# Two transformer blocks on one core: normalisations ahead of the feed-forward layers one token tile behind the other, and four smaller reorderings

## The reference

```python
# first block
x = layer_norm(ALPHA * x + mixed, ln_mix)            # "x1"
x = layer_norm(ALPHA * x + cross_attention(x), ln_x) # "x2"
x = layer_norm(ALPHA * x + conv_ffn(x), ln_ffn)      # "x3"
# second block
y = concat([mlstm(x), dilated_attention(x)]) @ w_out
x = layer_norm(ALPHA * x + y, ...)                   # "x4"
x = layer_norm(ALPHA * x + memory_cross_attention(x, mem), ...)  # "x5"
x = layer_norm(ALPHA * x + swiglu_ffn(x), ...)       # the output

def conv_ffn(x, w_in, conv_w, conv_b, w_out):
    gate, up = split(x @ w_in, 2)                    # 5632 columns each
    gate = causal_conv(gate, conv_w) + conv_b        # 3 taps
    return (silu(gate) * up) @ w_out
```

## Time and profile before

| | |
|---|---|
| median of three runs | 3367.18 us |
| time of the profiled execution | 3369.35 us |
| its span (first to last instruction) | 3367.5 us |
| mean granted TensorE clock | 0.987 of 2.4 GHz |
| PE busy | 3280.2 us, 97% |
| DVE busy | 1999.0 us, 59% |
| ACT busy | 1351.1 us, 40% |
| HBM traffic | 188 GB/s over the span |

### The profile page before, as it was taken

One profiled execution on the slowest core, in us unless ns is written; L12 is line 12 of the kernel. 1 busy time (PEld: TensorE's weight loads), 2 busy tenths in 40 slices (PEclk: granted clock), 3 DMA queues, 4 the chain that ended last, 5 costly groups with the idle time before them and its releaser, 6 DMA issues.

```text
span 3367.5 us, 43216 instructions
## 1 busy us (share of the span) xinstructions
PE 3280.2 (97%) x18465; PEld 2849.8 (85%) x18465; DVE 1999.0 (59%) x1606; ACT 1351.1 (40%) x888; POOL 0.2 (0%) x4
## 2 busy tenths in 40 slices
PE   8999999999989999999999989989999999999998
PEld 8988888887878888888889879789998888888887
DVE  6455666657576666665465665764445544545555
ACT  4333555433334444443333443333333444444332
POOL 0000000000000000000000000000000000000000
PEclk9999999999999999999999999999999999999999
DMA  7644555678436555555645544655546455565553
GB/s 261 210 163 150 184 198 215 219 255 294 154 109 202 185 195 180 186 203 195 215 171 179 180 146 172 213 180 175 164 162 212 150 188 189 183 199 187 193 194 137
DMA packets 309423, 635.58 MB, mean 189 GB/s; under 512 B 10888, under 2 KB 16820, under 8 KB 307124
## 3 DMA queue, kind: packets, MB, share of 16 engines
q1 hardware_dynamic: 296080, 587.50, 51.7%
q10 hardware_dynamic: 13220, 46.25, 3.7%
HBM read 618.51 MB, written 15.20 MB: 188 GB/s over the span
## 4 chain that ended last, share of the span: by engine, by line
PE 89%; DVE 6%; ACT 2%; issue 1%; DMA 1%; ACTq 0%; SPq 0%; DVEq 0%
PE ps L938 41%; PE ps L923 19%; PE ps L933 14%; PE ps L925 10%; PE ps L984 4%; DVE wlo L1373 2%; PE ps L988 1%; ACT whi L565 1%; DMA wraw<-in_w_in 1%; DVE m_t L1426 0%; DVE tok L1550 0%; DVE tok L1545 0%; DVE l_a L1963 0%; DVE alt_l L1426 0%; DVE l_s L1426 0%
## 5 line engine op out<-in xcount | busy, mean ns | idle before, releaser
L1373 DVE TENSOR_TENSOR wlo<-wraw,whi 128x2048 fp32r<-128x2048 f32 x549 | 1244.7, 2279 | 743.2 <-ACT whi L565 733.9
L565 ACT ACTIVATE whi<-wraw 128x2048 fp32r<-128x2048 f32 x549 | 1042.2, 1906 | 1470.5 <-PE ps L938 674.1
L923 PE MATMUL ps<-act_hl,whi 128*128 128x512 f32 x2816 | 978.9, 394 | 0.0
L925 PE MATMUL ps<-act_hl,wlo 128*128 128x256 f32 x2816 | 780.9, 277 | 0.0
L938 PE MATMUL ps<-whi,act_hl 128*128 128x512 f32 x2176 | 678.0, 393 | 0.7 <-DVE wlo L1373 0.7
L923 PEld LDWEIGHTS ps<-act_hl,whi 128*128 128x128 f32 x2816 | 529.0, 188 | 122.9
L925 PEld LDWEIGHTS ps<-act_hl,wlo 128*128 128x128 f32 x2816 | 529.4, 188 | 0.0
L938 PEld LDWEIGHTS ps<-whi,act_hl 128*128 128x128 f32 x2176 | 406.1, 188 | 85.2 <-issue 1.9
L933 PE MATMUL ps<-act_hl,whi 128*128 128x256 f32 (+1 forms) x2400 | 443.5, 287 | 13.6 <-DVE wlo L1373 9.6
L938 PE MATMUL ps<-wlo,act_hl 128*128 128x512 f32 x1088 | 424.4, 390 | 0.0
L933 PEld LDWEIGHTS ps<-act_hl,whi 128*128 128x128 f32 (+1 forms) x2400 | 378.6, 194 | 16.2 <-issue 13.9
(11 more groups left out here) (308 smaller groups left out, 2410.9 us busy)
## 6 DMA issues: line engine op xcount, KB each, us to landing
wraw<-in_w_in SPq DMA_DIRECT2D x156, 1024.0 KB, 5.3
wraw<-in_w SPq DMA_DIRECT2D x132, 1024.0 KB, 5.1
wraw<-in_ffn_in SPq DMA_DIRECT2D x88, 1024.0 KB, 5.0
wraw<-in_ffn_out SPq DMA_DIRECT2D x44, 1024.0 KB, 5.1
wraw<-in_w_branch SPq DMA_DIRECT2D x16, 1024.0 KB, 5.2
wraw<-in_w_mix_out SPq DMA_DIRECT2D x16, 1024.0 KB, 5.5
wraw<-in_w_out SPq DMA_DIRECT2D x16, 1024.0 KB, 5.1
wraw<-in_xk SPq DMA_DIRECT2D x16, 1024.0 KB, 5.1
```

Of the source, the lines that this page charges most:

```text
L565: act.activation(whi[:, slot, k, c], wraw[:, slot, k, c], ACT.Copy).then_inc(hi_done, 1)
L923: pe.matmul(o, whi[:, slot, k, c:c + P], hi[:, kc, :, :], start=first, stop=False, skip_group_check=True)
L925: ins = pe.matmul(o[:, 0:T], wlo[:, slot, k, c:c + P], hi[:, kc, 0, :], start=False, stop=stop, skip_group_check=True)
L1373: dve.tensor_tensor(wlo[:, slot, k, c], wraw[:, slot, k, c], whi[:, slot, k, c].bitcast(F32), ALU.subtract).then_inc(lo_done, 1)
```

## The change

It has five parts. (1) `norm` issues both tiles of quarter 1 ahead of `low` 0 (x1, x3, x4). (2) For x4 DVE rounds weights up to unit 362 ahead of `low` 0. (3) In the mLSTM the unit that stood between the transposes and `probs_kept` moves ahead of the wait for `l_s`, and in the dilated attention's first group the same for query tile 1. (4) For x2 and x5 the last output products go tile by tile (`tile_unit`): tile 0 of all of x2's columns 1 to 3 first, then tile 1, and of x5's last column the same after its first unit. The two tiles are normalised one behind the other, each in four quarters of 512x128, eight pieces instead of four, in three PSUM banks in turn (`FLIP_AT`). (5) The first gate block runs in two passes (`gate_apart`): first tile 0's columns of `whi` times high and low, which needs no `wlo`, for all four units, then tile 1's and the `wlo` products for both tiles. The warming matmuls ahead of x2 and x5 go. `hi` calls are regrouped to match.

```diff
@@ -619,6 +625,31 @@
+def tile_deviation(h):
+    mapping((rstd[:, h:h + 1], rstd[:, h:h + 1], ACT.Sqrt))
+def tile_high(dst, i):
+    q, h = i % NB, i // NB
+    bank = FLIP_AT[i % 3]
+    act.wait_ge(flipped, w.at("flipped"))
+    act.activation(dst[:, 4 * q:4 * q + 4, h * P:h * P + P],
+                   ps[:, bank:bank + UNIT].rearrange("p (s t) -> p s t", s=4), ACT.Copy).then_inc(high_ready, 1)
+def norm_apart(dst):
+    tile_deviation(0)
+    tile_high(dst, 0)
+    tile_high(dst, 1)
+    hi(1)
+    tile_high(dst, 2)
+    tile_deviation(1)
+    hi(1)
+    tile_high(dst, 3)
+    hi(1)
+    for i in range(4, 8):
+        tile_high(dst, i)
@@ -1000,6 +1031,26 @@
+def flip_tile(name, i):
+    q, h = i % NB, i // NB
+    bank = FLIP_AT[i % 3]
+    pe.wait_ge(normed, w.at("normed"))
+    if i >= 3:
+        pe.wait_ge(piece_ready, pieces(name, i - 2))
+    for c in range(CB):
+        x = turn(ps[:, bank + c * P:bank + c * P + P], tok[:, q, h, c * P:c * P + P])
+    x.then_inc(flipped, 1)
+def tile_unit(unit, h, hi, lo, bank, chunk, first, last):
+    slot = (unit - 1) % SLOTS
+    for k in range(CB):
+        for n, (wt, op) in enumerate(((whi, hi), (whi, lo), (wlo, hi))):
+            x = mm(ps[:, bank + h * UNIT:bank + h * UNIT + UNIT], op[:, chunk + k, h * P:h * P + P], wt[:, slot, k, :],
+                   first and k + n == 0, last and k == CB - 1 and n == 2)
+    return x
@@ -1160,15 +1211,45 @@
+def gate_apart(name):
+    base = w.now("unit")
+    both = [ps[:, s * UNIT:(s + 1) * UNIT].rearrange("p (x t) -> p x t", x=2) for s in range(CB)]
+    for u in range(4):
+        if u < 3:
+            flip_tile(name, u + 2)
+        pe.wait_ge(piece_ready, pieces(name, u + 1))
+        pe.wait_ge(hi_done, base + u + 1)
+        slot = (base + u) % SLOTS
+        for k in range(CB):
+            for s in range(CB):
+                mm(both[s][:, :, 0:P], whi[:, slot, k, s * P:s * P + P], act_hl[:, CB * u + k, :, 0:P],
+                   u + k == 0, False)
+    for u in range(4):
+        if u < 3:
+            flip_tile(name, u + 5)
+        pe.wait_ge(piece_ready, pieces(name, u + 5))
+        pe.wait_ge(lo_done, w.at("unit"))
+        slot = (base + u) % SLOTS
+        for k in range(CB):
+            for s in range(CB):
+                mm(both[s][:, :, P:T], whi[:, slot, k, s * P:s * P + P], act_hl[:, CB * u + k, :, P:T], False, False)
+                x = mm(both[s][:, 0, :], wlo[:, slot, k, s * P:s * P + P], act_hl[:, CB * u + k, 0, :], False,
+                       u + k == 2 * CB - 2)
+        x.then_inc(unit_done, 1)
...
-    def gate_up(turning=None):
+    def gate_up(first=False):
...
-        products(D_BLOCK, 4, act_hl, None, 0, first_of=first_of, turning=turning)
+        if first:
+            gate_apart(first_of)
+        else:
+            products(D_BLOCK, 4, act_hl, None, 0)
...
-    gate_up((first_of, EARLY))
+    gate_up(True)
@@ -1226,9 +1307,22 @@
 pe.wait_ge(operand, after("xa"))
-for cb in range(NB):
-    column(T_BLOCK, units=1, hi=alt_h, lo=alt_l)
-stay_warm(PC, 9)
+column(T_BLOCK, units=1, hi=alt_h, lo=alt_l)
+first = w.now("unit") + 1
+at = [w.now("block") % 2 * 1024, (w.now("block") + 1) % 2 * 1024, PC]
+for h in range(NT):
+    for c in range(3):
+        if h == 0:
+            pe.wait_ge(lo_done, first + c)
+            b = w.at("block")
+            if c < 2:
+                pe.wait_ge(block_saved, b - 2)
+            tile_unit(first + c, h, alt_h, alt_l, at[c], 0, True, True).then_inc(tile_done, 1)
+        else:
+            if c == 2:
+                flip_tile("x2", 0)
+                flip_tile("x2", 1)
+            tile_unit(w.at("unit"), h, alt_h, alt_l, at[c], 0, True, True).then_inc(unit_done, 1)
 ffn("x2")
@@ -1270,12 +1364,11 @@
         x.then_inc(result_ready, 1)
-        fill(behind_lstm, LSTM_FILL[g][1 + 2 * qt] - 1)
+        fill(behind_lstm, LSTM_FILL[g][1 + 2 * qt])
         pe.wait_ge(left_ready, w.at("left"))
...
         turn_probs(l_s, 2, n)
-        fill(behind_lstm, 1)
         probs_kept()
@@ -1296,13 +1389,13 @@
         if g == 0:
-            fill(behind_lstm, 3)
+            fill(behind_lstm, 3 + qt)
         else:
...
         turn_probs(d_s, 4, n)
-        if g == 0:
+        if g == 0 and qt == 0:
             fill(behind_lstm, 1)
@@ -1352,8 +1445,18 @@
 column(T_BLOCK)
-column(T_BLOCK)
-stay_warm(PC, 9)
+w.at("block")
+products(T_BLOCK, 1, act_h, act_l, PC, last=False)
+first = w.now("unit") + 1
+for u in range(3):
+    pe.wait_ge(lo_done, first + u)
+    x = tile_unit(first + u, 0, act_h, act_l, PC, CB * (u + 1), False, u == 2)
+x.then_inc(tile_done, 1)
+for u in range(3):
+    if u == 2:
+        flip_tile("x5", 0)
+        flip_tile("x5", 1)
+    tile_unit(w.at("unit"), 1, act_h, act_l, PC, CB * (u + 1), False, u == 2).then_inc(unit_done, 1)
 ffn("x5", by_tiles=True)
@@ -1538,15 +1641,15 @@
-def normal(name, t, q, signal, tiles=range(NT)):
+def normal(name, t, q, signal):
     c = slice(q * UNIT, (q + 1) * UNIT)
-    for h in tiles:
+    for h in range(NT):
         dve.scalar_tensor_tensor(t[:, q, h, :], t[:, q, h, :], mv[:, h, 0:1], gain_t[name][:, c],
...
         w.at("step")
-    for n, h in enumerate(tiles):
-        dve.wait_ge(dve_step, w.now("step") - len(tiles) + 1 + n)
+    for h in range(NT):
+        dve.wait_ge(dve_step, w.now("step") - 1 + h)
         x = dve.scalar_tensor_tensor(t[:, q, h, :], t[:, q, h, :], rstd[:, h:h + 1], bias_t[name][:, c],
@@ -1556,14 +1659,62 @@
     normal(name, t, 0, normed)
-    normal(name, t, 1, normed, (0,))
-    low(name, hi, dst, 0)
-    normal(name, t, 1, normed, (1,))
-    for q in range(1, NB):
+    for q in range(NB):
         if q < NB - 1:
...
         low(name, hi, dst, q)
+def tile_sum(cb, h, bank):
+    o = bank + h * UNIT
+    return dve.scalar_tensor_tensor(tok[:, cb, h, :], tok[:, cb, h, :], ALPHA, ps[:, o:o + UNIT], ALU.mult, ALU.add)
+def tile_statistics(cb, h):
+    link(dve.bn_stats(bst[:, h, 6 * cb:6 * cb + 6], tok[:, cb, h, :]))
+def tile_deviation(h):
+    link(dve.bn_aggr(mv[:, h, :], bst[:, h, :]))
+    to_act(dve.tensor_scalar(rstd[:, h:h + 1], mv[:, h, 1:2], EPS, None, ALU.add))
+    link(dve.reciprocal(rstd[:, h:h + 1], rstd[:, h:h + 1]))
+def tile_normal(name, h, which):
+    for q in which:
+        c, x = slice(q * UNIT, (q + 1) * UNIT), tok[:, q, h, :]
+        dve.scalar_tensor_tensor(x, x, mv[:, h, 0:1], gain_t[name][:, c], ALU.subtract, ALU.mult).then_inc(dve_step, 1)
+        w.at("step")
+    for n, q in enumerate(which):
+        c, x = slice(q * UNIT, (q + 1) * UNIT), tok[:, q, h, :]
+        dve.wait_ge(dve_step, w.now("step") - len(which) + 1 + n)
+        dve.scalar_tensor_tensor(x, x, rstd[:, h:h + 1], bias_t[name][:, c], ALU.mult, ALU.add).then_inc(normed, 1)
+def tile_low(name, hi, dst, i):
+    q, h = i % NB, i // NB
+    bank = FLIP_AT[i % 3]
+    c, t = slice(CB * q, CB * q + CB), slice(h * P, h * P + P)
+    dve.wait_ge(high_ready, w.at("high"))
+    tt(dst[:, c, t], four(ps[:, bank:bank + UNIT]), hi[:, c, t].bitcast(F32), ALU.subtract).then_inc(piece_ready, 1)
+    assert w.at("piece") == pieces(name, i + 1)
+def second_tile(name, unit):
+    ahead[0] = 0
+    tile_deviation(1)
+    tile_low(name, act_h, act_l, 2)
+    tile_low(name, act_h, act_l, 3)
+    tile_normal(name, 1, (0, 1))
+    tile_low(name, act_h, act_l, 4)
+    lo_to(unit + 1)
+    tile_low(name, act_h, act_l, 5)
+    tile_normal(name, 1, (2,))
+    lo_to(unit + 2)
+    tile_low(name, act_h, act_l, 6)
+    tile_normal(name, 1, (3,))
+    lo_to(unit + 3)
+    tile_low(name, act_h, act_l, 7)
@@ -1902,11 +2053,35 @@
-residuals(tok, (1, 1, 1, 1), 155)
+residuals(tok, (1,), 152)
+lo_to(152)
+at = [w.now("block") % 2 * 1024, (w.now("block") + 1) % 2 * 1024, PC]
+for c in range(3):
+    dve.wait_ge(tile_done, w.at("tile"))
+    link(tile_sum(c + 1, 0, at[c]))
+    tile_statistics(c + 1, 0)
+    if c == 0:
+        lo_to(153)
+ahead[0] = 0
+tile_deviation(0)
+dve.wait_ge(gains_in, gains_loaded("x2"))
+tile_normal("x2", 0, (0, 1))
+for c in range(2):
+    dve.wait_ge(unit_done, w.at("unit"))
+    w.at("block")
+    kept(tile_sum(c + 1, 1, at[c]))
...
-ahead[0] = 155
-norm("x2", tok, act_h, act_l, (0, 0, 0, 156))
+tile_low("x2", act_h, act_l, 0)
+tile_low("x2", act_h, act_l, 1)
+tile_normal("x2", 0, (2, 3))
+for c in range(2):
+    tile_statistics(c + 1, 1)
+dve.wait_ge(unit_done, w.at("unit"))
+w.at("block")
+kept(tile_sum(3, 1, PC))
+tile_statistics(3, 1)
+second_tile("x2", 153)
@@ -2068,7 +2243,7 @@
 ahead[0] = 0
-norm("x4", tok, alt_h, alt_l, (0, 363, 364, 0))
+norm("x4", tok, alt_h, alt_l, (362, 363, 364, 0))
 def keys():
@@ -2101,9 +2276,24 @@
-residuals(tok, (7, 1, 4, 4), 424)
-ahead[0] = 424
-norm("x5", tok, act_h, act_l, (0, 0, 0, 425))
+residuals(tok, (7, 1, 4), 424)
+lo_to(422)
+dve.wait_ge(tile_done, w.at("tile"))
+link(tile_sum(3, 0, PC))
+tile_statistics(3, 0)
+ahead[0] = 0
+tile_deviation(0)
+dve.wait_ge(gains_in, gains_loaded("x5"))
+tile_normal("x5", 0, (0, 1))
+tile_normal("x5", 0, (2,))
```

(28 more changed lines are left out.)

## The result

| | before | after |
|---|---|---|
| median (four runs each) | 3367.56 us | 3347.20 us |
| lowest to highest | 3366.68 to 3369.57 | 3345.36 to 3349.25 |
| profiled execution: time, span | 3369.35, 3367.5 us | 3347.13, 3345.2 us |
| mean granted clock | 0.987 | 0.993 |
| PE busy | 3280.2 us | 3280.6 us |

The ratio after to before is 0.9939 (95%: 0.9922 to 0.9956): 20.4 us gained where 36.4 were forecast, and outside the range. PE's idle time went as foreseen; its busy time ought to have shrunk with the stretches at a low clock, and did not.

A forecast was written before the change was run, and what follows sets the result against it. PE, busy for 97% of the span, was taken as the bound, with gains only in its idle time or low-clock matmuls. 3.5+2.9+11.1+8.1+0.7+3.6+6.5 = 36.4 us off 3367.2 gave 3330.8 us, range 3321 to 3342.

The forecast's parts named there:

- Part 1: Order of `norm` in x1 and x3: PE flips and starts its first unit sooner, 3.5 us in x1, 2.9 in x3.
- Part 2: x4: rounding weights up to unit 362 ahead of `low` 0 removes PE's 8.76 us wait; 11.1 us, range 9 to 11.1.
- Part 3: mLSTM and dilated group 0: units moved ahead of the transposes cover PE's waits; 8.1 us and 0.7 us.
- the walk-through: mLSTM group 1: events followed to the second answer products, expected at 2007.8 against 2015.79, 8.0 us sooner.
- Part 4: x2 and x5: split tiles with a two-pass gate block gain 3.6 us (1.9 to 5.3) and 6.5 (4.7 to 8.2).
- The charge of 1.7 us for the clock: x2 and x5: 1.7 us taken off each block's gain for low clock around the new waits.
- (b): Rival: weight loads not hidden behind 256-column matmuls, 64 extra loads a block in two blocks, 24 us, 3355 us; chance 0.02.
- (d): Rival, slower: two-strip matmuls stream at the plain f32 rate, 0.32 us more each, 82 us, 3413 us; chance 0.03.
- (a): Rival: only the repairs pay; waits of 4.7 and 3.4 us or lower clocks eat Part 4, 3340.9 us; chance 0.10.
- (c): Rival: a copy or `lo` behind moved units or rounds becomes the wait; half yield, 9.6 us less, 3340.4 us; chance 0.06.
- (e): Rival, better: the clock stays up through all shortened waits, all high ends, 44 us, 3323 us; chance 0.06.

The follow-up runs named there:

- e6: Kernel after plus eight transposes between first gate block and first up block of each layer, four runs on another chip: 3329.49 us.
- e5: Kernel after with no new edit, five runs on another chip: 3348.27 us.
- e3: Kernel after plus eight transposes between first gate block and first up block of each layer, one execution: 3330.19 us.
- e7: e6 with ACT's high copy of piece 3 put ahead of a weight copy instead of behind it: 3326.98 us.
- e11: Kernel before plus eight transposes ahead of the first up block in both layers: 3373.35 us, ratio 0.9994 to the kernel before.

## Why the prediction was wrong, and where it was right

**The step that failed** is what was held fixed. The sum costed the touched parts and took every other unit at its old duration; for the layers it says "nothing is given back there", and argues that with `lo` being in time, no wait appears. No wait did. But 168 units of D pairs behind the two gate blocks each took 0.107 us longer: 18 us. A sum over waits and counts can't see this. The sign was in the old trace, in x2's first gate block, in a unit that the prediction did not measure (PE's timeline of the kernel before):

```profile
997.28 0.48 PE L923 MATMUL ps<-act_hl,whi 128*128 128x512 f32 x1
...
1003.02 1.03 PE L988 MATMUL ps<-core,tok 128*128 128x128 f32 x8
```

This unit takes 5.74 us, and its pairs go round in threes, 350, 361, 349 ns: the slow rhythm, with 0.08 us more for the first pair behind the transposes. The prediction's own two numbers, 5.63 and 5.55 for a gate unit, look like the two rhythms and aren't. The 5.63 (from x5) is 16 pairs at a mean of 0.3467, with the same 0.08 for the first. Either way the difference asked for a look; the slow unit's, times the 84 units of a layer, would have given 9 us for each as a bound.

**With the rhythm kept (e6)** the kernel runs in 3329.49 us, 1.3 from the forecast, but that closeness is partly luck: the parts gained 41.8, not 36.4, and 1.6 us went to the added transposes and 1.5 to other stretches.

**Part 1** (3.5 and 2.9): 3.1 and 3.5; in e5's profile of the same kernel 4.4 and 1.3, so the nearness of each is partly luck, while the sum (6.6 and 5.6 for 6.4) holds better. One small wait is new, 0.24 us ahead of x3's first unit, for `low` 0. The second flip was forecast at 902.3 against a first flip at 899.7, 2.6 behind it; it came 2.56 behind (903.48 less 900.92), with an idle time of 1.49 us, forecast 1.5.

**Part 2** (11.1): 12.1 in the stretch, of which 11.0 lie in x4 itself (from the output product at 2153.75 and 2141.26 on) and 1.1 in dilated units ahead of it (19.2 us before, 18.0 after). Nothing new waits. The `wlo` wait is gone, and the flips follow each other without idle time.

**Part 3** (8.1 and 0.7): 10.3 together. The waits for `l_s` are gone, and ACT's copy shows as four waits of 0.5 us, as foreseen (0.69 in the group that had this order). Group 0 gained 0.9 for 0.4. From the start of group 1 to the second answer products (1964.42 to 2015.79 before, 1962.38 to 2005.19 after) it is 8.6, for the 8.0 of the walk-through, and 0.8 from there to the end of the stretch, for 0.7. The sum itself took 8.1 for both groups, where 8.0 and twice 0.2 are 8.4.

**Part 4** (3.6 and 6.5): 5.0 and 7.8. The chain of events was right in order: a first wait of 1.06 us (forecast 1.2), a second of 4.18 (4.7) for tile 1's quarter, behind a high copy that waits for a `hi`, and in x5 2.62 (3.4). The charge of 1.7 us for the clock was about right: behind x2's wait the transposes and the 32 strip matmuls start over 5.74 us (986.00 to 991.74) where the next four transposes and 32 matmuls take 4.27 (991.74 to 996.01), 1.5 us lost, and in x5 over 5.82 (2595.69 to 2601.51), 1.6 lost. In e5's profile x2's took 6.94 and its whole stretch 56.7 us, a gain of 3.8. What was over-stated is the waits, by 0.5 and 0.1 in x2 and 0.8 in x5; the rest of the 1.4 and 1.3 us was not traced. Windows of the kernel after, around the two waits, show the lowered granted clock (0.84 and 0.81):

```profile
984.00:995.00 11.00, 9.00 (x64) 9.01 (x65) 7.45 (x9) 2.23 (x3) 0.00 (x0) 0.84 0.27 87
2592.00:2600.00 8.00, 5.38 (x34) 5.17 (x34) 6.22 (x7) 3.33 (x4) 0.00 (x0) 0.81 0.01 2
```

**The rivals.** (b), weight loads not hidden, is refuted for this form, and the trace disagrees with the rule of the Trainium skill that stood beside it (TensorE: Matmul & The Clock Gate, "What overlaps and what doesn't"): in pass two a new 128x128 load and 256 columns follow each other every 0.120 us, 32 of them from 1004.55 to 1008.39. (d), slow strips: refuted by the same kind of rows, 16 strip matmuls starting at 979.66 have a joined record of 2.16 us, 0.12 apart with one overlapping end. (a) gave 3340.9, nearer to the truth than the forecast, for a wrong reason: part 4 did pay, 12.8 us. (c) and (e) did not come.

What stays open is what picks the rhythm. That the slow one comes with a longer pair of the same instructions, that it is held for a whole layer, and that a program with a few more transposes ahead of the layer can have the other, is shown. A rule that tells the rhythm from the stream is not: eight transposes were followed by the fast one in all eight layers that had them added (e3, e6, e7, e11), but the unit at 997.28 above is slow right behind eight. Weight loads, PSUM banks, the engine's queue and the place of the code were not tried one by one.

## What to carry to other kernels

When PE is busy for 97% of the time, list the start-to-start time of the commonest matmul form in every stretch before and after, also where nothing was changed: 0.0067 us a pair, in 168 units, took back over two fifths of what the change gained. If two values of it stand in one trace, treat the gap times the count as an uncertainty of the forecast, and try a few harmless instructions ahead of the loop. And put the small copy that PE is about to need ahead of a large one that it isn't: one swapped line gave 2.5 us.

## What the runs showed of the hardware

- A stream of 512- and 256-column matmuls, each with its weight load, at a granted clock of 1.00 and without idle time, runs at 0.3467 or at 0.3533 us a pair, and keeps its rhythm through a layer's 21 blocks, some 470 us. The steps of the fast one alternate (350, 343 ns), in e11's first layer they are 346, 347, 347; those of the slow one go round in threes (350, 361, 349). In the fast one the 512-column records last 392 to 395 ns in a stretch of ten, in the slow one 395 to 403. The T and F units show no such pair of values: in undisturbed stretches 0.2267 for 512 columns and 0.1200 for 256, in all profiles.
- Eight added transposes a layer (0.8 us each time) took 18.8 us off, 3348.27 to 3329.49, on one chip.
- A matmul over two strips of 128 columns of one PSUM and operand tile goes as fast as one of 256 columns in a row.
- Whether a wait of 1.5 us is followed by a stretch at a low clock differs between executions of the same kernel: the eight transposes behind x1's took 1.63 us in one and 1.09 in another, those behind x3's 1.09 and 1.97.
